# Forgetting attention in a four-layer transformer: the gate sums by DMA, heads in pairs, the output product between the last heads

## What is computed

```python
f_logit = jnp.einsum('bsd,dh->bhs', h, w_fg[j]) + b_fg[j][None, :, None]
log_f = jax.nn.log_sigmoid(f_logit.astype(jnp.float32))
cum = lax.cumsum(log_f, axis=2)
z = jnp.einsum('bhqd,bhkd->bhqk', qb, kb).astype(jnp.float32) * scale
decay = cum[:, :, q0:k_end, None] - cum[:, :, None, :k_end]
logits = jnp.where(s_idx <= t_idx, z + decay, -jnp.inf)
p = jax.nn.softmax(logits, axis=-1)
o = jnp.einsum('bhqk,bhkd->bhqd', p.astype(vb.dtype), vb)
x = x + gt_a[:, None, :] * rmsnorm(einsum(o, w_o[i]), g_mix_post[i])   # shortened
```

## Time and profile before

| | |
|---|---|
| median of 3 runs | 1562.66 us (1558.1 to 1564.45) |
| the profiled execution | 1563.33 us, of which its span 1562.1 us |
| busy, share of the span | PE 92%, PEld 82%, DVE 67%, ACT 47%, POOL 6% |
| read from HBM | 311.22 MB, 200 GB/s over the span |
| mean granted clock of PE | 0.943 of 2.4 GHz |
| chain of waits that ended last | PE 81%, DVE 8%, ACT 6%, issue 2%, POOL 2%, DMA 1% |

### The profile page before, as it was taken

One profiled execution on the slowest core, in us unless ns is written; L12 is line 12 of the kernel. 1 busy time (PEld: TensorE's weight loads), 2 busy tenths in 40 slices (PEclk: granted clock), 3 DMA queues, 4 the chain that ended last, 5 costly groups with the idle time before them and its releaser, 6 DMA issues.

```text
span 1562.1 us, 22095 instructions
## 1 busy us (share of the span) xinstructions
PE 1441.8 (92%) x8984; PEld 1278.9 (82%) x8984; DVE 1046.9 (67%) x1522; ACT 739.0 (47%) x1163; POOL 94.0 (6%) x137
## 2 busy tenths in 40 slices
PE   4898889999899997999988999988999989899998
PEld 3887689998688766999866775568999879799987
DVE  5777377786656675888845445847777488666653
ACT  3666365543643325555444444735444353454441
POOL 0034100000000000000001101210000000000000
PEclk9998989999999858999998998998999989999999
DMA  8865236488355552677743122135877648455650
GB/s 348 306 244 190 105 135 243 182 325 315 132 191 216 190 214 92 234 269 269 273 168 125 65 98 81 57 106 197 293 292 296 242 169 305 174 216 189 259 193 33
DMA packets 44277, 313.69 MB, mean 201 GB/s; under 512 B 4881, under 2 KB 5393, under 8 KB 6801
## 3 DMA queue, kind: packets, MB, share of 16 engines
q1 hardware_dynamic: 44176, 312.29, 53.9%
HBM read 311.22 MB, written 1.05 MB: 200 GB/s over the span
## 4 chain that ended last, share of the span: by engine, by line
PE 81%; DVE 8%; ACT 6%; issue 2%; POOL 2%; DMA 1%; SPq 0%; DVEq 0%; POOLq 0%; ACTq 0%
PE mat L450 15%; PE mat L451 15%; PE mat L452 15%; PE mat L477 7%; PE mat L479 7%; PE mat L481 7%; PE mat L689 2%; PE mat L690 2%; PE mat L691 2%; DVE raw L1218 2%; PE mat L654 1%; PE mat L655 1%; DVE wlo L1200 1%; PE mat L657 1%; PE mat L435 1%
## 5 line engine op out<-in xcount | busy, mean ns | idle before, releaser
L1200 DVE TENSOR_TENSOR wlo<-raw,whi 128x1024 fp32r<-128x1024 f32 x393 | 477.7, 1229 | 255.0 <-ACT whi L823 253.0
L450 PE MATMUL mat<-hHL,whi 128*128 128x256 f32 x1864 | 537.9, 289 | 13.3 <-DVE hHL L1272 10.4
L823 ACT ACTIVATE whi<-raw 128x1024 fp32r<-128x1024 f32 x393 | 408.7, 1054 | 284.8 <-PE mat L481 122.4
L451 PE MATMUL mat<-hHL,whi 128*128 128x256 f32 x1864 | 535.0, 287 | 0.0
L452 PE MATMUL mat<-hHL,wlo 128*128 128x256 f32 x1864 | 534.5, 287 | 0.0
L450 PEld LDWEIGHTS mat<-hHL,whi 128*128 128x128 f32 x1864 | 365.7, 196 | 16.8 <-issue 12.3
L451 PEld LDWEIGHTS mat<-hHL,whi 128*128 128x128 f32 x1864 | 365.6, 196 | 0.1
L452 PEld LDWEIGHTS mat<-hHL,wlo 128*128 128x128 f32 x1864 | 365.6, 196 | 0.0
L1218 DVE SCALAR_TENSOR_TENSOR raw<-raw,cB 128x1024 f32<-128x1024 f32 x192 | 237.3, 1249 | 7.3 <-DMA raw<-in_mod 7.2
L477 PE MATMUL mat<-whi,aHL 128*128 128x512 f32 x352 | 109.2, 391 | 0.0
L479 PE MATMUL mat<-wlo,aHL 128*128 128x512 f32 x352 | 108.5, 389 | 0.0
(11 more groups left out here) (208 smaller groups left out, 1756.2 us busy)
## 6 DMA issues: line engine op xcount, KB each, us to landing
raw<-in_mod SPq DMA_DIRECT2D x96, 1024.0 KB, 5.4
raw<-in_qkv SPq DMA_DIRECT2D x48, 1024.0 KB, 5.4
raw<-in_gate SPq DMA_DIRECT2D x44, 1024.0 KB, 4.9
raw<-in_up SPq DMA_DIRECT2D x44, 1024.0 KB, 5.4
raw<-in_down SPq DMA_DIRECT2D x44, 1024.0 KB, 5.8
raw<-in_wo SPq DMA_DIRECT2D x16, 1024.0 KB, 5.5
cB<-in_crow SPq DMA_DIRECT2D x3, 512.0 KB, 8.0
x<-in_x SPq DMA_DIRECT2D x1, 1024.0 KB, 8.6
```

Source lines behind the costliest of these rows:

```text
L450: pe.matmul(o, wh[:, k, :], hH[:, k, :], start=(k == 0), stop=False)
L451: pe.matmul(o, wh[:, k, :], hL[:, k, :], start=False, stop=False)
L823: act.activation(whi[:, n % NSPL, :], raw[:, f % NRAW, 1024 * h:1024 * h + 1024], ACT.Copy).then_inc(s_hi, 1)
L1200: dve.tensor_tensor(out=wlo[:, n % NSPL, :], in0=raw[:, f % NRAW, 1024 * h:1024 * h + 1024], in1=whi[:, n % NSPL, :].bitcast(f32), op=ALU. ...
```

## The change

1. The gate's sums and the mask leave PE. SP writes `ncum` to a buffer in HBM and reads each head's row back into all 128 partitions (16 transfers of 128 KB, into `xn` and `tmp`, which are free then). POOL fills the masked places with -1e30 by two `affine_select` a head. DVE adds this to the scores and takes the extremum in one instruction a query tile (`tensor_tensor_reduce`, listed as ISA, with a short second one that reads the accumulator), written negated to SBUF. ACT takes the exponentials from there.
2. Scores and values are issued for two heads at once, alternating between rows 0 to 63 and 64 to 127 of the array (scores), or between the two halves of its columns (values). The (1,0) and (1,1) blocks are one matmul of 256 columns. Scores go on even steps, values on odd ones.
3. Two parts of wo follow each of PE's steps 13 to 19. For this, banks move, wo is in groups `[1, 1, 1, 1]`, the gate's rows of layer 1's mixer come with the last two halves of wo, and ACT and DVE split one half at each of the steps 16 to 19 instead of four afterwards.
4. The mod steps are placed anew: 16 instead of 40 go with layer 1's heads, more with the feed-forward nets and with layer 2's heads.

```diff
     _spread([(0, 2), (0, 3), (0, 4)], heads(0, 0, 18))
-    _spread([(0, 5)], halves(START["ffn", 0] + 8, START["ffn", 0] + 44))
-    _spread([(1, 1), (1, 0)], halves(START["ffn", 0] + 44, START["ffn", 0] + 64))
-    _spread([(1, 2), (1, 3), (1, 4), (2, 0), (2, 2)], heads(1, 0, 20))
-    _spread([(1, 5), (2, 3)], halves(START["ffn", 1] + 8, START["ffn", 1] + 46))
-    _spread([(2, 1)], halves(START["ffn", 1] + 46, START["ffn", 1] + 62))
-    _spread([(2, 4)], heads(2, 4, 20))
-    _spread([(2, 5), (3, 1), (3, 0), (3, 2)], halves(START["ffn", 2] + 8, START["ffn", 2] + 60))
-    _spread([(3, 3), (3, 4)], halves(START["mix", 3] + 6, START["ffn", 3] - 4))
+    _spread([(0, 5), (1, 1)], halves(START["ffn", 0] + 8, START["ffn", 0] + 46))
+    _spread([(1, 0), (1, 2), (1, 3)], halves(START["ffn", 0] + 46, START["ffn", 0] + 66))
+    _spread([(1, 4), (1, 5)], heads(1, 0, 16))
+    _spread([(2, 1)], halves(START["ffn", 1] + 8, START["ffn", 1] + 46))
+    _spread([(2, 0), (2, 2)], halves(START["ffn", 1] + 46, START["ffn", 1] + 64))
+    _spread([(2, 3), (2, 4)], heads(2, 4, 20))
+    _spread([(2, 5), (3, 1), (3, 0), (3, 2), (3, 3)], halves(START["ffn", 2] + 8, START["ffn", 2] + 64))
+    _spread([(3, 4)], halves(START["mix", 3] + 6, START["ffn", 3] - 4))
     _spread([(3, 5)], halves(START["ffn", 3] + 8, START["ffn", 3] + 44))
...
-            ROWS_BEFORE[_n + 2 * _c] = (_l, _p, _c)
-            ROWS_AFTER[_n + 2 * _c + 5] = (_l, _p, _c)
+            if (_l, _p) == (1, 2):
+                ROWS_BEFORE[HALF["wo", 1, 6 + _c]] = (_l, _p, _c)
+            else:
+                ROWS_BEFORE[_n + 2 * _c] = (_l, _p, _c)
+                ROWS_AFTER[_n + 2 * _c + 5] = (_l, _p, _c)
             ROWS_AT[_l, _p, _c] = len(ROWS_AT) + 1
...
+        def forget_w(h):
+            return ws[h % 3]
+        def forget_mask(h):
+            return ws[3 + h % 3]
+        def forget_sums(h):
+            if h < 8:
+                return xn[:, h // 4, 256 * (h % 4):256 * (h % 4) + 256]
+            return tmp[:, (0, 1, 4, 5)[h // 2 - 4], 256 * (h % 2):256 * (h % 2) + 256]
...
+                if item == ("w", CHUNK_OF[HALF["q", 1, 2, 0]][0]):
+                    sp.wait_ge(s_fg, 5)
+                    sp.dma_start(A["sums"], ncum[:, :]).then_inc(s_sums, 16)
+                    sp.wait_ge(s_sums, 16)
+                    for h in range(H):
+                        sp.dma_start(forget_sums(h), A["sums"][h:h + 1, :].to_broadcast([P, S])).then_inc(s_cumb[h // 4], 16)
...
+                    if (k, t) == (0, 0) and l == 1:
+                        pe.wait_ge(s_max, 24)
+                        pe.wait_ge(s_w, H + 9)
...
-                token_product(HALF["wo", l, 0], KT, [1, 1, 2], oH, oL, o_ready)
+                wo = token_parts(HALF["wo", l, 0], KT, [1, 1, 1, 1] if l == 1 else [1, 1, 2], oH, oL, o_ready)
+                if l < 2:
+                    tensor_causal(l, wo)
...
+                for _ in wo:
+                    pass
...
+                if l == 1 and at >= 13:
+                    next(wo)
+                    next(wo)
...
+        def forget_bank(h):
+            return h % 2 if h < 12 else (4, 7)[h % 2]
+        def forget_turn_bank(h):
+            return 2 + h % 2 if h < 9 else 6
         def tensor_forgetting(step):
             h = step - 4
-            if 0 <= h < H:
+            if h >= 0 and h % 2:
                 pe.wait_ge(s_w, H + h + 1)
-                values(1, h, ws[h % 6])
+                if h > 1:
+                    pe.wait_ge(s_o, 8 + h // 2)
+                for c, t0, i, start, stop in ((0, 0, 0, True, True), (128, 128, 0, True, False), (256, 128, 1, False, True)):
+                    for g in (h - 1, h):
+                        hp = 64 * (g % 2)
+                        m = pe.matmul(mat[hp:hp + 64, 5, t0:t0 + P], v01[:, i, 64 * g:64 * g + 64], forget_w(g)[:, c:c + P],
+                                      start=start, stop=stop)
+                m.then_inc(s_val, 2)
             h = step - 3
             if 0 <= h < H:
-                p, b = zs[h % 4], 2 + h % 2
+                p, b = zs[h % 4], forget_turn_bank(h)
                 pe.wait_ge(s_nrm, 3 * h + 3)
-                if h > 1:
-                    pe.wait_ge(s_w, H + h - 1)
+                before = [g for g in range(h) if forget_turn_bank(g) == b]
+                if before:
+                    pe.wait_ge(s_w, H + before[-1] + 1)
                 for c in (0, 128, 256):
                     m = pe.transpose(bank(b)[:, c:c + P], p[:, c:c + P], ident[:, :])
                 m.then_inc(s_turn, 1)
             h = step
-            if h < H:
-                hp, ht, b = 64 * (h % 2), h // 2, h % 2
-                q, k = qT[hp:hp + 64, ht, :], kT[hp:hp + 64, ht, :]
-                eh = ident[0:H, h:h + 1].to_broadcast([H, P])
+            if h < H and h % 2 == 0:
+                ht = h // 2
                 if h % 4 == 0:
                     pe.wait_ge(s_qk, 8 + 2 * (h // 4) + 2)
                 if h == 0:
                     pe.wait_ge(s_v, 4)
-                    pe.wait_ge(s_msk, 2)
-                    pe.wait_ge(s_fg, 5)
-                if h > 1:
-                    pe.wait_ge(s_exp, 2 * (h - 2) + 2)
-                for c, t0, s0 in ((0, 0, 0), (128, 128, 0), (256, 128, 128)):
-                    dst = bank(b)[:, c:c + P]
-                    pe.matmul(dst, q[:, t0:t0 + P], k[:, s0:s0 + P], start=True, stop=False)
-                    m = pe.matmul(dst, eh, ncum[:, s0:s0 + P], start=False, stop=(c == 128))
-                    if c != 128:
-                        m = pe.matmul(dst, ident[:, :], msk[:, :], start=False, stop=True)
-                m.then_inc(s_sc, 1)
+                if h in (2, 4, 6, 8, 10, 14):
+                    pe.wait_ge(s_max, 2 * (h - 1) + 2)
+                for c, t0, n in ((0, 0, 128), (128, 128, 256)):
+                    for g in (h, h + 1):
+                        hp = 64 * (g % 2)
+                        m = pe.matmul(bank(forget_bank(g))[:, c:c + n], qT[hp:hp + 64, ht, t0:t0 + P], kT[hp:hp + 64, ht, 0:n],
+                                      start=True, stop=True)
+                        if c:
+                            m.then_inc(s_sc, 1)
...
-                hi(4)
+                if l != 1:
+                    hi(4)
+                else:
+                    gate_taken(1, 2, 0)
+                    gate_taken(1, 2, 1)
...
+                if l == 1 and at >= 16:
+                    hi(1)
...
-                if h >= 6:
-                    act.wait_ge(s_val, H + h - 5)
-                act.activation(ws[h % 6], bank(2 + h % 2)[:, 0:384], ACT.Copy).then_inc(s_w, 1)
+                if h >= 3:
+                    act.wait_ge(s_val, H + h - 2 + (h % 2 == 1))
+                act.activation(forget_w(h), bank(forget_turn_bank(h))[:, 0:384], ACT.Copy).then_inc(s_w, 1)
             h = step - 1
             if 0 <= h < H:
-                p, b = zs[h % 4], h % 2
-                if h >= 4:
-                    act.wait_ge(s_turn, h - 3)
+                p = zs[h % 4]
                 act.wait_ge(s_max, 2 * h + 2)
-                act.activation(p[:, 0:128], bank(b)[:, 0:128], ACT.Exp, bias=forget_stat(h, 0),
+                act.activation(p[:, 0:128], p[:, 0:128], ACT.Exp, bias=forget_stat(h, 0), scale=-1.0,
                                accum_out=forget_stat(h, 2)).then_inc(s_exp, 1)
-                act.activation(p[:, 128:384], bank(b)[:, 128:384], ACT.Exp, bias=forget_stat(h, 1),
+                act.activation(p[:, 128:384], p[:, 128:384], ACT.Exp, bias=forget_stat(h, 1), scale=-1.0,
                                accum_out=forget_stat(h, 3)).then_inc(s_exp, 1)
         def norm_stat(g):
...
-                lo(4)
+                if l != 1:
+                    lo(4)
...
+                if l == 1 and at >= 16:
+                    lo(1)
...
             if h < H:
-                b = h % 2
+                p, z, y = zs[h % 4], bank(forget_bank(h)), forget_mask(h)
                 dve.wait_ge(s_sc, H + h + 1)
-                dve.tensor_reduce(forget_stat(h, 0), bank(b)[:, 0:128], AX.X, ALU.max, negate=True).then_inc(s_max, 1)
-                dve.tensor_reduce(forget_stat(h, 1), bank(b)[:, 128:384], AX.X, ALU.max, negate=True).then_inc(s_max, 1)
+                dve.wait_ge(s_bm, h + 1)
+                if h >= 4:
+                    dve.wait_ge(s_turn, h - 3)
+                for i, cs in enumerate((slice(0, 128), slice(128, 384))):
+                    dve.tensor_tensor_reduce(out=p[:, cs], in0=z[:, cs], in1=y[:, cs], op0=ALU.add, op1=ALU.min, scale=-1.0,
+                                             scalar=-NEG, accum_out=forget_stat(h, i)).then_inc(s_max, 1)
...
-            pool.wait_ge(s_mk, H)
-            pool.tensor_scalar(msk[:, :], ones[:, :], -1.0, None, ALU.add).then_inc(s_msk, 1)
-            pool.wait_ge(s_msk, 1)
-            pool.affine_select(out=msk[:, :], in_=msk[:, :], compare_op=ALU.is_ge, fill=NEG, base=0, pattern=[[-1, P]],
```

(18 more changed lines are left out.)

22 lines of the change are left out of this document (13 added, 9 removed).

## The result

| | before | changed |
|---|---|---|
| median | 1563.56 us (4 runs) | 1515.88 us (1512.4 to 1522.62, 4 runs) |
| the profiled execution, its span | 1563.33, 1562.1 us | 1512.4, 1511.1 us |

What follows compares the result with a forecast made beforehand. PE was taken to bound the kernel, mostly with small matmuls in layer 1's mixer. The terms -30.7 - 27.9 + 2.4 + 1 + 3 + 3.5 = -48.7 took 1563.3 to 1514.6 us, own range 1505 to 1527, 8 in 10 1496 to 1538.

Steps and rivals of the forecast that it cites:

- steps 0 to 11, sums included: Layer 1's heads: paired scores gain 30.7 us (39.7 removed, 9.0 added); the sums' transfers cost 1.
- tail to the end of token tile 0: Layer 1's steps 12 to 19 with wo: 33.9 us at the full clock, 27.9 less, and 2.4 of waits.
- I take 1.5, since both halves are one shape: Layer 1's pairs of scores: 1.5 us each, six times 0.22 with seams, nothing added for changing halves.
- rival 1: Layer 1's heads: two heads run side by side in the array, 12 us less, 1503 us; chance 0.27.
- SP's queue, +1 (0 to 5): Layer 1's heads: the sums' issues delay chunks, and PE's step 2 waits; +1 us, from 0 to 5.
- Waits in the tail, +2.4: Layer 1: 1.0 us at step 12 for head 9's scaling, 1.1 at step 19 for gate rows, small hand-overs.
- rival 3: Layer 1's tail stays at half clock: some 30 us more, 1544 us; chance 0.04.
- Layer 0's down product, +3: 24 mod steps over 20 halves, from 16; transfers fall 9 us behind: +3 us, from 0 to 12.
- layer 1's net "at nothing": Layer 1's feed-forward net: at most 1.9 chunks for two halves of down, covered by the lead, no cost.
- Layer 2's heads, +3.5: Eight more mod steps, one in every step, 0.41 us each: +3.5 us, from 2.5 to 6.
- DVE as cover, and POOL at 0: Layer 1's steps 0 to 11: DVE busy 42 of 56 us; POOL's 14 us of selects add 0.
- rival 2: Weights late in layer 0's down product, or sums and DVE late in layer 1: 17 us more, 1531; chance 0.15.

Runs made afterwards that it cites:

- e12: The changed kernel run once more without an edit: 1514.1 us, ratio 0.967 to the kernel before.
- e5_same_half: The changed kernel with both heads of a pair in the same half of the array, values one head after the other: 1524.4 us, ratio 0.974.
- e6: The changed kernel with the chunk of k issued before SP waits for `ncum`: 1511.0 us, ratio 0.965 to the kernel before.
- e4: The changed kernel with wo multiplied after step 19 again, and its last four halves split afterwards: 1527.0 us, ratio 0.978 to the kernel before.
- e8: The changed kernel with another table of mod steps, moving four vectors to other halves: 1504.5 us, ratio 0.962 to the kernel before.
- e2: The changed kernel with the old table of mod steps (40 instead of 16 in layer 1's heads): 1530.8 us, ratio 0.980 to the kernel before.
- e11: The changed kernel without POOL's selects, the causal mask left out: 1515.7 us, ratio 0.968 to the kernel before.

## Why the prediction was right

It was right in the time (1514 forecast, 1515.9 measured) and in the mechanism of most of its terms. That the time fits within 2 us is luck in part. The pairs were priced 11 us too dear, and 5 us of slow clock in the old steps 0 to 11 were taken to stay; waits, and slow clock behind them, that the sum did not have took most of that back. The last column is the same kernel in e12, against the same execution of before.

| term | forecast | changed | e12 |
|---|---|---|---|
| steps 0 to 11, sums included | -30.7 + 1 | -35.8 (86.4 to 50.6) | -34.4 (to 52.0) |
| tail to the end of token tile 0 | -27.9 + 2.4 | -26.8 (61.8 to 35.0) | -29.1 (to 32.7) |
| layer 0's net | +3 | +2.9 | +5.9 |
| layer 1's net | 0 | +3.2 | +5.2 |
| layer 2's mixer | +3.5 | +3.1 | +2.7 |
| all else | 0 | +2.5, of it 2.4 ahead of layer 0's net, where the same line shows 0.1 to 3.4 in the other runs | +1.6 |
| sum | -48.7 | -50.9 | -48.1 |

**Scores and values.** The step "I take 1.5, since both halves are one shape" failed: 0.85 for the scores and 0.81 for the values. In steps 0 to 11 that is 6 x 0.65 + 4 x 0.69 = 3.9 + 2.8 us less than forecast, in the tail 2 x 0.65 + 4 x 0.69 = 4.1. The mechanism of rival 1 was true, and I had its ends on paper (0.75 for side by side), with 0.27. What speaks for the low price was in the diff: the operands stand at `hp = 64 * (g % 2)`, and consecutive matmuls alternate. The Trainium skill, "TensorEngine Tiling (Array Packing)", Key Properties, says that different tiles can load weights and multiply in parallel; the trace agrees, 0.85 against 1.50 us.

**The clock in steps 0 to 11.** e5_same_half is in effect the kernel I forecast, with pairs at 1.50 and 1.46 us, and its windows, 58.5 and 37.2 us, lie near my 56.7 and 36.3. Yet this does not prove the working. The forecast took matmuls at the full clock off a stretch of 86.4 us that held 5.1 us of slow clock, and so kept these; in e5 they are gone, and 4.1 us of waits and 3.4 of slow clock stand in their place, where the sum had 1. For the changed kernel the same count is 56.7 - 6.7 (pairs) - 5.1 (old slow clock) + 3.9 + 1.7 - 1 (waits and slow clock, for the 1 of the sum) = 49.5 us, and 50.6 were measured; 1.1 stay open.

**Rival 1's time, 1503,** still did not come. Its 12 us were nearly right (9.7 in e5's mixer), but they were taken off a sum that lacked other costs: 4.3 us or more for the sums instead of 1, 3.2 in layer 1's net, and the 2.4 ahead of layer 0's net.

**SP's queue, +1 (0 to 5).** The order of events was as forecast, and even the landing of the chunk, moved by the 5 us by which all of layer 1 came later. Two things were left out: between head 0's and head 1's fused instruction DVE has a mod pass and a split (1.22 + 1.30 us), so that the wait was 3.4; and behind this wait PE's clock fell. Together they are 4.3 us by e6 against the changed kernel and 5.7 against e12: at the upper end of the bounds given, or just outside.

**Waits in the tail, +2.4.** One of the two came, at its place: head 9's scaling at step 12, at 2.6 instead of 1.0 us. PE's own step 11 took 1.3 us instead of the 2.0 I had, as its values too were cheaper. And the way from PE's last half of k (503.44) to the transposes of step 12 (507.40) took 4.0 us instead of 3.0, because two pieces were left out: ACT's copy of that half ahead of the split (0.6 with the hand-over) and DVE's split of an output behind its own (0.3). No mod pass has a part in it: behind the one of this step DVE stood idle for 0.93 us until ACT's split was done. A slow stretch followed, 2.8 us. The other wait (second gate rows at step 19) came to nothing: the trace has no wait of PE there. So the tail came out right because errors met in it: 33.9 us of work less 4.1 for the pairs, plus 2.6 of wait and 2.8 of slow clock, are 35.2, and 35.0 were measured. In e12, without the slow stretch, it was 32.7.

**The clock in the tail.** The full clock was right from 513.60 on, and e4 shows that it is wo between the heads that holds it: without it the tail runs at the half clock of rival 3, but at a third of its price (10 us for 30): some 4 us more of PE's busy time and 6 more of waits (0.7 of these at step 2).

**Layer 0's down product, +3.** Wrong in kind, and right in size by luck (2.9, but 5.9 in e12): the forecast's wait was for `wlo` near the end. What waits is PE's second gate rows, for a copy of ACT that stands behind splits that wait for a chunk. This is also why **layer 1's net "at nothing"** failed, with 3.2 and 5.2 us: the lead of split halves covers late chunks for the product, but not for the copy that stands in the same queue.

**Layer 2's heads, +3.5:** right step by step, 3.72 us each (3.73 forecast from the earlier trace rows), and e8 takes it back to 3.32 to 3.44.

**DVE as cover, and POOL at 0:** right. DVE was busy for 39.2 of 50.6 us where 42 were forecast, and e2 shows that the 24 mod steps taken out of the heads were needed there (28 us). POOL's selects were sized wrong, without harm: they were busy for 27.4 us instead of 14, most of it beside DVE, and e11 shows that they cost nothing. The count of mod passes in steps 0 to 11 was a little off too, 22 before and 11 now instead of 24 and 12, and rival 2's parts (9, 4 and 3 us over the terms of the sum) add up to 16 us, not 17.

## What to carry to other kernels

Price the wait with what may follow it: here an idle stretch of PE of some 3 us brought 1.4 to 3.4 us of slow clock in most cases and none in others, so dense work put between short, waiting steps can be worth more than its own length. And look for slow clock in the stretch that is to be shortened, before its length is carried over into a sum. When work is moved out of a stage that is to get faster, test it in both kernels: the same table was worth 15 us in one and cost 15 in the other. And look in each engine's program for small steps (a copy of gate rows, the maxima of a head) that stand behind a step fed by a transfer: the lead of buffered data doesn't cover those.

## What the runs showed of the hardware

- Two fp32 matmuls in different halves of the array (rows 0 to 63 and 64 to 127, or the two halves of its columns) run at once, also when one head is issued after the other: a pair of scores took 0.85 us in turn and 0.87 in series, a pair of values 0.81 and 1.08; with both heads in one half they took 1.50 and 1.46.
- After 3.4 and 2.6 us without work PE ran at a granted clock of 0.63 over 4.7 us and 0.51 over 6.2 us, behind 10 us at 1.00 each. The length of the wait did not decide it. The fourteen traces have 40 waits of PE of 1.8 to 4.6 us for DVE in layer 1's heads or for the gate rows' copy, each behind 10 us at 1.00: behind 29 of them the clock fell to 0.5 within 7 us, behind 11 (of 1.8 to 3.6 us) it stayed at 1.00. In the kernel before it fell three times to 0.5 while PE had no wait at all (458, 502 and 527 us).
- A POOL select of 128 columns takes 0.29 us alone and 1.09 beside DVE's passes with two inputs in SBUF; DVE's split takes 1.25 us on average beside it and 1.22 without (e11). So the two exclude each other, and here POOL is the one that waits. The Trainium skill, "SBUF — State Buffer", in the section on the two sides, says that whichever starts first holds the ports for its whole instruction; the select at 461.66 began inside DVE's pass of 461.37 to 462.59 and ended just behind it, at 462.75.
- A transfer of 1 KB from HBM to each of 128 partitions was issued every 0.47 us and did not hold the queue; the chunk of 1 MB behind 16 of them took 7.5 us to land.
